# The last LayerNorm of a residual layer, spread over more engines

## What is computed

```python
def _layernorm(x, g, b):
    mu = jnp.mean(xf, axis=-1, keepdims=True)
    var = jnp.mean(jnp.square(xf - mu), axis=-1, keepdims=True)
    return (xf - mu) * lax.rsqrt(var + LN_EPS) * g + b
...
    h = x * (1.0 + scale[:, 2, None, :]) + shift[:, 2, None, :]
    y = _swiglu(h, ffn2_w_in[l], ffn2_w_out[l])
    x = _layernorm(ALPHA * x + 0.5 * gate[:, 2, None, :] * y, post_ln_g[l, 2], post_ln_b[l, 2])
return x
```

## Time and profile before

| | us |
|---|---|
| median of 3 runs | 994.31 |
| lowest and highest run | 993.32, 994.58 |
| profiled execution, its own time | 994.68 |
| its span, first to last instruction | 992.9 |

### The profile page before, as it was taken

One profiled execution on the slowest core, in us unless ns is written; L12 is line 12 of the kernel. 1 busy time (PEld: TensorE's weight loads), 2 busy tenths in 40 slices (PEclk: granted clock), 3 DMA queues, 4 the chain that ended last, 5 costly groups with the idle time before them and its releaser, 6 DMA issues.

```text
span 992.9 us, 10623 instructions
## 1 busy us (share of the span) xinstructions
PE 956.1 (96%) x4130; PEld 761.7 (77%) x4130; DVE 509.4 (51%) x718; ACT 373.5 (38%) x546; POOL 241.8 (24%) x209
## 2 busy tenths in 40 slices
PE   4999999999999999999999999999999999999992
PEld 3788888888878887777766786888888888788881
DVE  5956767545456754767655477722322222234225
ACT  3743232342222332655484447532332323212213
POOL 0021111111107221328834363611111111052110
PEclk8899999999999999999999999999999999999996
DMA  9836565656653744113511112323232232223202
GB/s 363 330 106 207 180 207 191 191 185 197 201 174 124 246 145 128 53 64 106 127 43 43 43 64 83 101 93 106 88 103 92 100 106 80 96 80 97 78 17 85
DMA packets 37474, 127.20 MB, mean 128 GB/s; under 512 B 4016, under 2 KB 4144, under 8 KB 37424
## 3 DMA queue, kind: packets, MB, share of 16 engines
q1 hardware_dynamic: 37424, 126.52, 38.5%
HBM read 123.36 MB, written 2.10 MB: 126 GB/s over the span
## 4 chain that ended last, share of the span: by engine, by line
PE 94%; DVE 3%; ACT 2%; issue 1%; DMA 0%; SPq 0%; DVEq 0%; ACTq 0%
PE bank L549 28%; PE bank L550 28%; PE bank L551 28%; PE bank L854 2%; PE bank L831 1%; PE bank L657 1%; PE bank L620 1%; PE bank L621 1%; PE bank L597 1%; PE bank L612 1%; DVE x L1283 1%; PE bank L842 1%; DVE w_lo L933 0%; DMA x<-xT 0%; PE bank L586 0%
## 5 line engine op out<-in xcount | busy, mean ns | idle before, releaser
L933 DVE TENSOR_TENSOR w_lo<-raw,w_hi 128x1024 fp32r<-128x1024 f32 x159 | 217.3, 1373 | 301.8 <-ACT w_hi L925 301.3
L549 PE MATMUL bank<-h_hi,w_hi 128*128 128x512 f32 x730 | 286.4, 392 | 0.0
L551 PE MATMUL bank<-h_hi,w_lo 128*128 128x512 f32 x730 | 284.4, 390 | 0.0
L550 PE MATMUL bank<-h_lo,w_hi 128*128 128x512 f32 x730 | 284.3, 390 | 0.0
L925 ACT ACTIVATE w_hi<-raw 128x1024 fp32r<-128x1024 f32 x159 | 162.3, 1032 | 207.9 <-PE bank L551 206.8
L1661 POOL TENSOR_TENSOR a_lo<-act_t,a_hi 128x512 fp32r<-128x512 f32 x44 | 58.5, 1329 | 428.1 <-ACT a_hi L1009 428.1
L549 PEld LDWEIGHTS bank<-h_hi,w_hi 128*128 128x128 f32 x730 | 137.2, 188 | 29.3 <-issue 1.1
L551 PEld LDWEIGHTS bank<-h_hi,w_lo 128*128 128x128 f32 x730 | 137.2, 188 | 28.7
L550 PEld LDWEIGHTS bank<-h_lo,w_hi 128*128 128x128 f32 x730 | 137.2, 188 | 28.3 <-issue 0.5
L549 PE MATMUL bank<-a_hi,w_hi 128*128 128x512 f32 x352 | 141.1, 401 | 0.0
L551 PE MATMUL bank<-a_hi,w_lo 128*128 128x512 f32 x352 | 139.5, 396 | 0.0
(11 more groups left out here) (252 smaller groups left out, 1003.7 us busy)
## 6 DMA issues: line engine op xcount, KB each, us to landing
raw<-wunits SPq DMA_DIRECT2D x145, 512.0 KB, 3.2
ada_ring<-ada_w SPq DMA_DIRECT2D x56, 512.0 KB, 4.5
ada_first<-ada_w SPq DMA_DIRECT2D x16, 512.0 KB, 8.9
raw<-wunits SPq DMA_DIRECT2D x16, 384.0 KB, 2.9
x<-xT SPq DMA_DIRECT2D x4, 512.0 KB, 5.7
outT<-x SPq DMA_DIRECT2D x8, 256.0 KB, 2.0
K<-k_rope SPq DMA_DIRECT2D x2, 512.0 KB, 8.0
c_act<-c_rows SPq DMA_DIRECT2D x1, 512.0 KB, 8.0
```

The costliest lines, as they stand in the source:

```text
L549: mm(out, lh, rh, start=first, stop=False)
L550: mm(out, lh, rl, start=False, stop=False)
L551: return mm(out, ll, rh, start=False, stop=last)
L933: nc.vector.tensor_tensor(lo, raw[:, slot, 0:width], hi.bitcast(F32), SUB).then_inc(s_lo, 1)
```

## The change

Only the last norm changes; the two norms before it run through the old code.

- **Root.** ScalarE forms the first value of the root with one function, `Abs_reciprocal_sqrt`, read straight from bank 7; the preload fetches the table of that function. VectorE's Newton step stays, with its intermediate values in PSUM banks 0 and 1 and its result in `rstd`, in SBUF. ScalarE then copies `rstd` to bank 7.
- **Centring.** `shift` now holds minus the mean. VectorE centres tile 0, GpSimd tiles 1 to 3. For tiles 4 to 7 TensorE adds `x[m]` and `shift` in PSUM banks 2 to 5, as two fp32 products each with the identity `ident` (part of `cols`); the product with `x[4]` is put ahead of `stats_end`.
- **Scaling.** VectorE multiplies seven tiles in the order 4, 5, 0, 1, 2, 6, 7; GpSimd multiplies tile 3.
- **Affine parts.** ScalarE takes tiles 4, 5, 0, 2; GpSimd 3, 1, 6; VectorE 7.
- **Stores.** SyncE's order is 4, 5, 3, 0, 1, 2, 6, 7.

```diff
+LAST_POOL = (1, 2, 3)
+LAST_PE = (4, 5, 6, 7)
+LAST_SCALED = (4, 5, 0, 1, 2, 6, 7)
+LAST_ACT_OUT = (4, 5, 0, 2)
+LAST_POOL_OUT = (1, 6)
+LAST_STORED = (4, 5, 3, 0, 1, 2, 6, 7)
...
+            def last_centred():
+
+                pe.wait_ge(s_mc, 3)
+                for b, m in zip(CENTRED_BANK, LAST_PE):
+                    if m != LAST_PE[0]:
+                        mm(bank[b][:], ident, x[:, m, :], start=True, stop=False)
+                    mm(bank[b][:], ident, shift[:], start=False, stop=True).then_inc(s_pc, 1)
...
                 if f == 1:
+                    mm(bank[CENTRED_BANK[0]][:], ident, x[:, LAST_PE[0], :], start=True, stop=False)
                     stats_end(p + 1)
+                    last_centred()
...
+            def last_root():
+
+                act.wait_ge(s_st[3], 1)
+                fn(tmp[:], bank[MEAN[3]][:], ACT.Square).then_inc(s_rq[3], 1)
+                fn(shift[:], bank[MEAN[3]][:], ACT.Copy, scale=-1.0).then_inc(s_mc, 1)
+                act.wait_ge(s_rv[3], 1)
+                fn(y0[:], bank[SQR[3]][:], ACT.Abs_reciprocal_sqrt).then_inc(s_rq[3], 1)
+                act.wait_ge(s_rv[3], 4)
+                fn(bank[SQR[3]][:], rstd[:], ACT.Copy).then_inc(s_rq[3], 1)
...
-                preload(2 + f, ACT.Ln)
+                preload(2 + f, ACT.Abs_reciprocal_sqrt if f else ACT.Ln)
...
+            def last_norm():
+
+                mean, square = bank[MEAN[3]], bank[SQR[3]]
+                z, w = (bank[b] for b in ROOT_BANK)
+                dve.wait_ge(s_st[3], 2)
+                dve.wait_ge(s_rq[3], 1)
+                stt(square[:], square[:], SUM_EPS, tmp[:], ADD, SUB).then_inc(s_rv[3], 1)
+                dve.wait_ge(s_mc, 3)
+                centre(3, 0, mean)
+                dve.wait_ge(s_rv[3], 1)
+                dve.wait_ge(s_rq[3], 2)
+                tt(z[:], square[:], y0[:], MUL).then_inc(s_rv[3], 1)
...
+                stt(w[:], z[:], -0.5, y0[:], MUL, MUL).then_inc(s_rv[3], 1)
...
+                stt(rstd[:], w[:], 1.5, y0[:], ADD, MUL).then_inc(s_rv[3], 1)
...
+                for m in LAST_SCALED:
...
+                        scaled = tt(x[:, m, :], bank[CENTRED_BANK[LAST_PE.index(m)]][:], rstd[:], MUL)
...
-            for m in POOL_LAST:
+            pool.wait_ge(s_mc, 3)
+            for m in LAST_POOL:
+                tt(x[:, m, :], x[:, m, :], shift[:], ADD).then_inc(s_pf, 1)
+            pool.wait_ge(s_pf, len(LAST_POOL))
+            pool.wait_ge(s_rv[3], 4)
+            m = LAST_POOL[-1]
+            tt(x[:, m, :], x[:, m, :], rstd[:], MUL).then_inc(s_pf, 1)
```

More of the change, by code:

```diff
@@ L76 @@
 AFFINE_STEP = 4
-POOL_LAST = (1, 4, 6)
+LAST_POOL = (1, 2, 3)
[4 more added lines that the diff above has]
+LAST_STORED = (4, 5, 3, 0, 1, 2, 6, 7)
 S_FILL = S_UQ0 + 1
@@ L321, in y_bank @@
             return bank[OUT_BANK[m] if p == 2 else Y0 + m % 2]
+        ROOT_BANK, CENTRED_BANK = (0, 1), (2, 3, 4, 5)
         OPEN_BANK = {1: (0, 1, 2, 3), 2: (0, 1, 4, 5)}
@@ L411, in build @@
         s_pf, s_mc = sem("pool_finished"), sem("mean_copied")
+        s_pc = sem("centred_by_matmul")
         s_cen = [None] + [sem(f"centred{p}") for p in range(1, 4)]
@@ L531, in _ @@
                 unit(n)
-            for m in range(KD):
-                if m in POOL_LAST:
-                    sp.wait_ge(s_pf, POOL_LAST.index(m) + 1)
+            for m in LAST_STORED:
+                if m in LAST_ACT_OUT:
+                    sp.wait_ge(s_hh[3], LAST_ACT_OUT.index(m) + 1)
+                elif m == LAST_POOL[-1]:
+                    sp.wait_ge(s_pf, len(LAST_POOL) + 2)
+                elif m in LAST_POOL_OUT:
+                    sp.wait_ge(s_pf, len(LAST_POOL) + 3 + LAST_POOL_OUT.index(m))
                 else:
-                    sp.wait_ge(s_hh[3], m + 1 - sum(n < m for n in POOL_LAST))
+                    sp.wait_ge(s_nx[3], len(LAST_SCALED) + 1)
                 sp.dma_start(outT[m], x[:, m, :]).then_inc(s_out, 16)
@@ L1041, in ffn @@
                 square(p, KD - 1)
-                root(p, 1, MX + LEAD if f == 0 else None)
+                if f == 0:
+                    root(p, 1, MX + LEAD)
+                else:
+                    last_root()
             act.wait_ge(s_c, 16)
@@ L1192, in _ @@
             ffn(F2, 1, 3, a_hi2)
[L1193 to L1196, removed]
+            for m in LAST_ACT_OUT:
+                act.wait_ge(s_nx[3], LAST_SCALED.index(m) + 1)
                 fn(x[:, m, :], x[:, m, :], ACT.Identity, scale=cols[:, C_LNG + 3 * KD + m:C_LNG + 3 * KD + m + 1],
@@ L1271, in root @@
                 stt(bank[SQR[p]][:], tmp[:], 1.5, y0[:], ADD, MUL).then_inc(s_rv[p], 1)
+            def last_norm():
[9 more added lines that the diff above has]
+                tt(z[:], square[:], y0[:], MUL).then_inc(s_rv[3], 1)
+                dve.wait_ge(s_rv[3], 2)
+                stt(w[:], z[:], -0.5, y0[:], MUL, MUL).then_inc(s_rv[3], 1)
+                dve.wait_ge(s_rv[3], 3)
+                stt(rstd[:], w[:], 1.5, y0[:], ADD, MUL).then_inc(s_rv[3], 1)
+                dve.wait_ge(s_rv[3], 4)
+                for m in LAST_SCALED:
+                    if m == 0:
+                        dve.wait_ge(s_cen[3], 1)
+                        dve.wait_ge(s_rq[3], 3)
+                        scaled = tt(x[:, m, :], x[:, m, :], square[:], MUL)
+                    elif m in LAST_POOL:
+                        dve.wait_ge(s_pf, LAST_POOL.index(m) + 1)
+                        scaled = tt(x[:, m, :], x[:, m, :], square[:], MUL)
+                    else:
+                        dve.wait_ge(s_pc, LAST_PE.index(m) + 1)
+                        scaled = tt(x[:, m, :], bank[CENTRED_BANK[LAST_PE.index(m)]][:], rstd[:], MUL)
+                    scaled.then_inc(s_nx[3], 1)
+                m, c = LAST_SCALED[-1], 3 * KD + LAST_SCALED[-1]
+                dve.wait_ge(s_nx[3], len(LAST_SCALED))
+                ts(x[:, m, :], x[:, m, :], cols[:, C_LNG + c:C_LNG + c + 1],
+                   cols[:, C_LNB + c:C_LNB + c + 1], MUL, ADD).then_inc(s_nx[3], 1)
             def centre(p, m, mean):
@@ L1425, in ffn @@
                     plain_low(p, KD - 1)
-                root(p, 2, MX + LEAD if f == 0 else None)
-                normalise(p, MX if f == 0 else None)
+                if f == 0:
+                    root(p, 2, MX + LEAD)
+                    normalise(p, MX)
+                else:
+                    last_norm()
             for i in range(BN_PARTS):
@@ L1765, in _ @@
             ffn(1, 3, a_hi2, a_lo2)
-            for m in POOL_LAST:
+            pool.wait_ge(s_mc, 3)
[5 more added lines that the diff above has]
+            tt(x[:, m, :], x[:, m, :], rstd[:], MUL).then_inc(s_pf, 1)
+            for m in (LAST_POOL[-1], *LAST_POOL_OUT):
                 c = 3 * KD + m
-                pool.wait_ge(s_nx[3], m + 1)
+                if m == LAST_POOL[-1]:
+                    pool.wait_ge(s_pf, len(LAST_POOL) + 1)
+                else:
+                    pool.wait_ge(s_nx[3], LAST_SCALED.index(m) + 1)
                 ts(x[:, m, :], x[:, m, :], cols[:, C_LNG + c:C_LNG + c + 1],
```

## The result

| | before | after |
|---|---|---|
| median, us | 993.49 (5 runs, 993.32 to 994.58) | 988.91 (5 runs, 988.56 to 989.24) |
| ratio, 95% interval | | 0.995 (0.9938 to 0.9961) |
| profiled execution, own time | 994.68 | 989.24 |
| its span | 992.9 | 987.5 |
| start of the last residual | 972.83 | 972.46 |

The forecast was 989.1 with a range of 988.0 to 991.0. Its sum took 5.2 us off the profiled execution. The executions differ by 5.44, of which 0.37 lies ahead of the last residual, where nothing was changed, and 5.03 in the tail. I use the tail from here on, since it leaves out what differs from run to run ahead of it. In later sets of runs the kernel before came at a median of 993.80 (16 runs) and 993.97 (9 runs), so by medians the change is worth 4.6 to 5.1.

A forecast was written before the change was run, and what follows sets the result against it. The prediction took the tail to be bound by VectorE's operation count behind a serial root. Root 1.95 plus spread 3.25 gave 5.2 us off, 989.5 from the profiled execution, adjusted to the runs' median 989.1; range 988.0 to 991.0.

The forecast's parts named there:

- The bound of the tail: After the last residual to the span's end: VectorE's count of operations behind a serial root, 19.3 us from 973.6.
- The root: Last norm: one function replaces Ln, table load and Exp; Newton step starts 1.95 us earlier and ends at 979.19.
- rival 4: ScalarE's new root function brings a table load after all, 1.28 us before the first store: 990.4; chance 0.03.
- The open term: VectorE operations reading one bank and writing another might each take a tenth more, 0 to 0.3 us in sum.
- TensorE's last bank: Centring by identity products at 0.86 us each: tile 7's bank ready at 982.2.
- Rival 1: TensorE's clock falls under the identity products, 1.71 us each instead of 0.86: time 991.5; chance 0.07.
- VectorE's last tile: Tile 7, after seven multiplications stepping by 0.61 us and its affine part, ready at 984.0 to 984.4.
- Rival 2: GpSimd and VectorE shut each other out, GpSimd's operations taking 2.27 us: time 992.8, no tellable change; chance 0.05.
- The exception that the prediction names: Under the shared-port rule, only VectorE's affine part of tile 7 could be held; priced 0.43 to 0.80 us.
- The stores: Stores limit the end: first issued at 980.76, seven more landing by 0.64 us each, the last at 987.4.
- Rivals 3 and 5: Final stores: 3, no overlap, each awaits the previous landing, 998.9, chance 0.02; 5, queueing without loss, 988.0, chance 0.05.
- The sum: Whole gain: 5.2 us off the span, 1.95 from the root and 3.25 from the spread of eight tiles.

The follow-up runs named there:

- e12: The changed kernel with TensorE's seven remaining identity products held back until the Newton step is done; tail 18.89 us against 15.04.
- e7: The changed kernel with four unused VectorE multiplications put before the multiplication of tile 7; tail 16.10 us against 15.04.
- e8: The changed kernel without the Newton step, the function's value used as the root; tail 14.77 us against 15.04.
- e11: The changed kernel, Newton step kept, with the sharing out of tiles and store order of e9; tail 15.13 us, ratio to before 0.995.
- e10: e8 with SyncE's store order alone changed to 4, 5, 0, 3, 2, 1, 6, 7; tail 14.09 us against 14.77.
- e9: e8 with tiles shared out and stored by when they are centred, VectorE multiplying all eight; 986.99 us, ratio to before 0.9931.

## Why the prediction was right

- **The bound of the tail** was VectorE's count of operations behind a serial root, and the two experiments with one part each show both. Their shares were booked differently from what they are alone: 1.95 for the root holds only once the subtractions have left VectorE (0.95 without).
- **The root** was ready 6.43 after the last residual's start; the forecast was 979.19 - 972.83 = 6.36. Of the 0.07, 0.06 is a second wait on VectorE ahead of the first Newton operation. No load came back (rival 4). The open term, operations that read a bank and write one, was bounded by 0 and 0.3: they take 0.71 where 0.70 was taken, 0.03 in sum. (The prediction counts four; the list has three, since the last reads a bank and writes SBUF.)
- **TensorE's last bank** was to be ready at 9.37 by the same clock; the last product ends at 9.38. Rival 1 did not occur, PEclk stayed at 1.00. Its price kept the lower level to the end; in e12 the clock came back after 3.4 us under the products.
- **VectorE's last tile** was to be ready at 11.2 to 11.6, and was at 11.32, the affine part at 0.55 between its bounds of 0.43 and 0.80.
- **GpSimd** took 1.24 to 1.27 a two-tensor operation against 1.30. Rival 2 did not occur, because every two-tensor operation of VectorE beside it had an operand in a bank. The exception that the prediction names, tile 7's affine part, takes 0.55, as in e7, where GpSimd has finished; in e8 and e11, where GpSimd's last operation is further from its end, it takes 0.73 and 0.67. None of this reached the end of the changed kernel.
- **The stores.** First issue 8.02 against 7.93, last landing 3.0 after its issue against 3.2, rate 402 to 407 GB/s against 408. The last store is issued at 11.6 and not 11.4, since SyncE takes longer for an issue; that and the shorter landing cancel, as the queue, and not the last issue, fixes the landing. Rivals 3 and 5 are out: stores overlap, but queue. The 358 GB/s that DMA: Bandwidth & Descriptors of the Trainium skill (Where 436 GB/s comes from) names for the HBM side would have put the end 0.6 later; the measured rate decides against it.
- **The sum**: tail 14.87 forecast, 15.04 measured. The median moved by 4.58 and not by 5.2, mostly because the median of the kernel before came out at 993.49 with more runs, where 994.31 had been given; the medians of the changed kernel and the forecast differ by 0.2.

## What to carry to other kernels

Once the end of a kernel is spread over all engines, price its stores as a queue: the last byte leaves at the first store's time plus the number of stores by their rate, and whatever makes the tiles behind the first has slack that can be measured. In such a queue a tile that holds up finished ones near the front costs nearly all of its lateness (0.68 for some 0.86, e8 against e10), and one that is late at the end only what goes beyond its slack (1.06 of 2.4, e7). Keep one operand of VectorE in PSUM wherever GpSimd works beside it, and look at what an engine does meanwhile before booking a shorter chain as gained.

## What I had not expected

- A store of 128 KB from 64 partitions took the DMA engines 0.83 of the time of one of 256 KB from 128: 202 GB/s at 0.87 busy against 407 at 1.06.
- After a pause of 3.8 us TensorE's clock stayed at the lower level only for about two products (3.4 us), and returned under fp32 products with the identity.
- SyncE's issue of a store takes 0.33 at the median in the kernel before, 0.46 in the changed kernel, up to 0.55, and 0.60 with half stores. Stores that haven't landed aren't enough to lengthen it, since e9 and e11, which issue while earlier stores are under way, show 0.33 at the median; the cause stays open.
- Root and spread give 0.96 more together than the sum of each alone, because the spread takes away two of the three subtractions that VectorE did between the variance and the Newton step.
